# First block of x scaled in halves, late transposes by turns, last gain product on GpSimd: the start and the end of a one-core decoder kernel

## What is computed

```python
def rmsnorm(x, g):
    y = x * lax.rsqrt(jnp.mean(x * x, axis=-1, keepdims=True) + EPS)
    return y * g

h = rmsnorm(x, attn_norm_g)
proj = h @ w_in                     # conv, q, k, v and gate columns
...                                 # conv branch, windowed attention, gates, w_o, residual
h2 = rmsnorm(x, mlp_norm_g)
x = x + square(relu(h2 @ w_up)) @ w_down
out = rmsnorm(x, final_norm_g)      # 512 x 1024
```

## Time and profile before

| | us |
|---|---|
| median of 3 runs (lowest, highest) | 748.97 (748.92, 749.09) |
| the profiled execution | 749.23 |
| its span in the trace | 747.5 |
| TensorE busy | 740.1 (99% of the span) |
| VectorE busy | 658.7 (88%) |
| ScalarE busy | 429.3 (57%) |
| GpSimd busy | 86.0 (12%) |

### The profile page before, as it was taken

How to read it: one execution, slowest core, us unless ns; L and a number is a source line. 1 busy time by engine, 2 the same in 40 slices (tenths; PEclk the granted TensorE clock), 3 DMA queues, 4 the chain that set the end, 5 groups by cost and what they waited for, 6 DMA issues and landing times.

```text
span 747.5 us, 10674 instructions
## 1 busy us (share of the span) xinstructions
PE 740.1 (99%) x4194; PEld 649.9 (87%) x4194; DVE 658.7 (88%) x766; ACT 429.3 (57%) x555; POOL 86.0 (12%) x119
## 2 busy tenths in 40 slices
PE   8999999999999999999999999999999999999997
PEld 8898888888888888888888899889988999899985
DVE  6997788989899687989999999998699879986998
ACT  6773555553644557564658776654465455545556
POOL 1610000111122101010100101010101010100102
PEclk9999999999999999999999999999999999999999
DMA  9898223161247987778767847777677768676703
GB/s 325 240 299 275 76 65 105 57 168 58 84 133 238 307 226 200 191 225 200 250 169 178 215 121 214 175 196 198 170 188 199 179 171 216 173 202 181 208 1 114
DMA packets 68948, 134.41 MB, mean 180 GB/s; under 512 B 2653, under 2 KB 18085, under 8 KB 68901
## 3 DMA queue, kind: packets, MB, share of 16 engines
q1 hardware_dynamic: 48880, 85.23, 33.9%
q0 software_dynamic: 19808, 48.25, 30.0%
q10 hardware_dynamic: 212, 0.28, 0.1%
HBM read 127.43 MB, written 6.32 MB: 179 GB/s over the span
## 4 chain that ended last, share of the span: by engine, by line
PE 98%; DMA 1%; ACT 0%; DVE 0%; SPq 0%; issue 0%; ACTq 0%
PE pair L1094 46%; PE pair L1049 22%; PE pair L790 6%; PE pair L792 6%; PE pair L791 6%; PE pair L916 5%; PE pair L837 2%; PE pair L812 1%; PE pair L811 1%; PE pair L821 1%; DMA xn<-in_x 1%; PE pair L851 1%; PE pair L943 0%; PE pair L945 0%; PE pair L944 0%; PE pair L1000 0%
## 5 line engine op out<-in xcount | busy, mean ns | idle before, releaser
L1406 ACT ACTIVATE high<-home_raw 128x2048 fp32r<-128x2048 f32 x91 | 174.3, 1916 | 148.1 <-PE pair L1094 102.4
L2058 DVE TENSOR_TENSOR home_lo<-home_raw,high 128x2048 fp32r<-128x2048 f32 x91 | 208.5, 2291 | 34.4 <-ACT high L1406 34.1
L1094 PE MATMUL pair<-high,s_hi_tile 128*128 128x512 f32 x440 | 110.4, 391 | 0.0
L1094 PE MATMUL pair<-high,s_lo_tile 128*128 128x512 f32 x440 | 109.9, 390 | 0.0
L1094 PE MATMUL pair<-home_lo,s_hi_tile 128*128 128x512 f32 x440 | 109.7, 390 | 0.0
L1094 PEld LDWEIGHTS pair<-home_lo,s_hi_tile 128*128 128x128 f32 x440 | 82.4, 188 | 17.5 <-DVE home_lo L2058 0.4
L1094 PEld LDWEIGHTS pair<-high,s_lo_tile 128*128 128x128 f32 x440 | 82.4, 188 | 17.1
L1094 PEld LDWEIGHTS pair<-high,s_hi_tile 128*128 128x128 f32 x440 | 81.7, 188 | 17.4 <-ACT pair L1501 0.5
L790 PE MATMUL pair<-h,wgt 128*128 128x512 f32 x192 | 76.7, 399 | 0.0
L792 PE MATMUL pair<-h,wgt 128*128 128x512 f32 x192 | 75.0, 391 | 0.0
L791 PE MATMUL pair<-h,wgt 128*128 128x512 f32 x192 | 74.9, 390 | 0.0
(11 more groups left out here) (236 smaller groups left out, 1130.1 us busy)
## 6 DMA issues: line engine op xcount, KB each, us to landing
home_raw<-in_w_up SPq DMA_DIRECT2D x16, 1024.0 KB, 5.3
home_raw<-in_w_down SPq DMA_DIRECT2D x16, 1024.0 KB, 5.1
raw<-in_w_in SPq DMA_DIRECT2D x26, 512.0 KB, 4.9
home_raw<-in_w_up POOLq DMA_DIRECT2D x12, 1024.0 KB, 8.3
home_raw<-in_w_down POOLq DMA_DIRECT2D x12, 1024.0 KB, 8.5
home_raw<-in_w_in POOLq DMA_DIRECT2D x7, 1024.0 KB, 8.6
home_raw<-in_w_in SPq DMA_DIRECT2D x7, 1024.0 KB, 6.2
home_raw<-in_w_conv_out SPq DMA_DIRECT2D x4, 1024.0 KB, 5.2
```

What stands on the lines that cost most here:

```text
L1094: last = mm(pair[region(s, i)][:, b, :], a_[:, k, b * P:(b + 1) * P], w[:, k, :], start=(fresh and kind == 0 and k == 0), stop=(kind == 2 ...
L1406: a(high[n % 2][:, :], home_raw[home_of(s, name)][:, :], ACT.Copy).then_inc(m_hi, 1)
L2058: v.tensor_tensor(home_lo[home][:, :], home_raw[home][:, :], f32(high[n % 2][:, :]), ALU.subtract).then_inc(m_lo, 1)
```

## The change

Six edits, none of which changes what is computed:

1. x block 0 is scaled in two halves. VectorE's order is now: share of block 0, reciprocal and first half of block 0, share of block 1, second half of block 0, both halves of block 1.
2. The first transposes go block 0's four pairs, then block 1's four pairs, where before the blocks alternated from the third pair on.
3. The low part of M1's weight is made in three instructions (rows 0 and 1, row 2, row 3) where before it was two of two rows; N2's stays at two. TensorE waits and orders the third kind to match.
4. Block 3 is scaled in its two halves with the low part of tile 7 between them; tiles 4 to 6 come before.
5. The late transposes go (2,0) (2,1) (2,2) (3,0) (3,1) (2,3) (3,2) (3,3), and each pair of block 2 waits only for its own two tiles (`h_ready` 2n + 2).
6. At the end, the gain product of block 3 moves from VectorE to GpSimd, behind the two that it does; the early half of block 1 is scaled on VectorE (tensor_scalar) right behind block 1's late half, and no longer on ScalarE; block 3's late half is made and stored in two pieces of 256 columns, so SP issues eight stores.

```diff
-XN_PARTS = ((0, D), (0, D // 2, D), (0, D), (0, D // 2, D))
+XN_PARTS = ((0, D // 2, D), (0, D // 2, D), (0, D), (0, D // 2, D))
+        LOW_ROWS = {M1: ((0, 1), (2,), (3,)), N2: ((0, 1), (2, 3))}
+        def late_size(b):
+            return 256 if b == TB - 1 else 512
...
# SP
+            for b in range(TB):
+                for e in range(512 // late_size(b)):
+                    sp.wait_ge(out_late, b + e + 1)
+                    store(b, 512 * (1 - early(b)) + late_size(b) * e, late_size(b))
+                if b < TB - 1:
+                    sp.wait_ge(out_early[b], 1)
+                    store(b, 512 * early(b), 512)
+            sp.wait_ge(out_done, 16 * (2 * TB + 1))
...
# GpSimd
             gain(0)
             gain(1)
+            gain(3)
...
# TensorE
-            for b, n in ((0, 1), (1, 0), (0, 2), (1, 1), (0, 3), (1, 2), (1, 3)):
+            for b, n in ((0, 1), (0, 2), (0, 3), (1, 0), (1, 1), (1, 2), (1, 3)):
                 x_pair(b, n)
...
             def late_transposes():
-                pe.wait_ge(h_ready, 8)
-                x_transposes(2)
-                x_transposes(3)
+                for b, n in ((2, 0), (2, 1), (2, 2), (3, 0), (3, 1), (2, 3), (3, 2), (3, 3)):
+                    if b == 2:
+                        pe.wait_ge(h_ready, 2 * n + 2)
+                    x_pair(b, n)
...
# ScalarE
             def scale_early(b):
-                if b < 2:
-                    act.wait_ge(gained, b + 1)
-                else:
-                    act.wait_ge(gained_late, 1)
+                act.wait_ge(gained, 3 if b == 3 else b + 1)
...
             root_of(2)
-            scale_early(1)
             root_of(3)
...
# VectorE
             share_of_squares(0)
+            scale_x(0, (0,))
             share_of_squares(1)
-            scale_x(0)
-            scale_x(1)
+            scale_x(0, (1,))
+            scale_x(1, (0, 1))
...
-            q_low_half(M1, 0)
-            q_low_half(M1, 1)
-            scale_x(2)
+            for e in range(3):
+                q_low_rows(M1, e)
+            scale_x(2, (0,))
             share_of_squares(3)
-            for k in range(4, 8):
+            for k in range(4, 7):
                 tile_low(0, k)
-            scale_x(3)
+            scale_x(3, (0,))
+            tile_low(0, 7)
+            scale_x(3, (1,))
...
+            def scale_early_1():
+                dve.wait_ge(gained, 2)
+                r = res[:, 1, 512 * early(1):512 * early(1) + 512]
+                v.tensor_scalar(r, r, rms3[:, 2, 1:2], None, ALU.mult).then_inc(out_early[1], 1)
...
             factor(1)
-            gain(3)
             scale_late(1)
+            scale_early_1()
```

More of the change, by code:

```diff
@@ L403, in build @@
         ss3_ready, fin_step = sem("ss3_ready"), sem("fin_step")
-        gained, gained_late = sem("gained"), sem("gained_late")
+        gained = sem("gained")
         out_early, out_late = [sem(f"out_early{b}") for b in range(TB)], sem("out_late")
@@ L645, in _, with store @@
             sp.dma_start(gfin[:, :], bass.AP(final_norm_g.tensor, 0, [[0, P], [1, D]])).then_inc(gfin_in, 16)
[L646 to L653, removed]
-                else:
+            def store(b, c0, n):
+                sp.dma_start(out[rows_of(b), c0:c0 + n], res[:, b, c0:c0 + n]).then_inc(out_done, 16)
+            for b in range(TB):
[3 more added lines that the diff above has]
+                if b < TB - 1:
                     sp.wait_ge(out_early[b], 1)
-                    store(sp, b, early(b))
-            sp.wait_ge(out_done, 16 * 2 * TB)
+                    store(b, 512 * early(b), 512)
+            sp.wait_ge(out_done, 16 * (2 * TB + 1))
         @block.gpsimd
@@ L702, in _ @@
             store_sum(M6)
-            pool.wait_ge(q_low, 5)
+            pool.wait_ge(q_low, 6)
             add_q(N4, 1, 0, q_t4_in)
@@ L854, in x_pair @@
                     last.then_inc(xt_ready, 1)
-            def x_transposes(b):
-                for n in range(4):
-                    x_pair(b, n)
             def idle_transposes(n):
@@ L888, in q_product @@
                     elif early_:
-                        order = [(k, f) for e in range(2) for f in range(4) for k in (2 * e, 2 * e + 1)]
+                        order = [(k, f) for rows in LOW_ROWS[i] for f in range(4) for k in rows]
                     else:
@@ L896, in q_product @@
                         elif kind == 2:
-                            pe.wait_ge(q_low, at_ + 3)
+                            pe.wait_ge(q_low, at_ + 4)
                         if i in HS:
@@ L913, in q_product @@
                                 pe.wait_ge(h_ready, 4 * at_ + k + 1)
-                            elif k % 2 == 0:
-                                pe.wait_ge(q_low, 2 * at_ + k // 2 + 1)
+                            elif any(k == rows[0] for rows in LOW_ROWS[i]):
+                                pe.wait_ge(q_low, 3 * at_ + [rows[0] for rows in LOW_ROWS[i]].index(k) + 1)
                         last = mm(acc[:, f, :], w[:, k, f * P:(f + 1) * P], a_[:, k, :],
@@ L1783, in share_of_squares, with scale_x, q_low_rows @@
                                        ).then_inc(share_done, 1)
[L1785 to L1797, removed]
+            def scale_x(b, parts):
+                if 0 in parts:
+                    dve.wait_ge(root_done, b + 1)
+                    v.reciprocal(rms[:, 1, b:b + 1], rms[:, 0, b:b + 1]).then_inc(rms_step, 1)
+                    dve.wait_ge(rms_step, b + 1)
+                for e in parts:
+                    c = slice(*XN_PARTS[b][e:e + 2])
+                    v.tensor_scalar(xn[:, b, c], xn[:, b, c], rms[:, 1, b:b + 1], None, ALU.mult).then_inc(xn_ready, 1)
+            def q_low_rows(i, e):
+                at_, rows = Q_ORDER.index(i), LOW_ROWS[i][e]
+                c = cols(512 * rows[0], 512 * len(rows))
+                dve.wait_ge(q_high, 4 * at_ + rows[-1] + 1)
                 v.tensor_tensor(q_lo[i][:, c], q_raw[i][:, c], f32(q_hi[at_ % 2][:, c]), ALU.subtract).then_inc(q_low, 1)
@@ L1841, in _ @@
                 tile_low(0, k)
-            q_low_half(M1, 0)
-            q_low_half(M1, 1)
-            scale_x(2)
+            for e in range(3):
+                q_low_rows(M1, e)
+            scale_x(2, (0,))
             share_of_squares(3)
-            for k in range(4, 8):
+            for k in range(4, 7):
                 tile_low(0, k)
-            scale_x(3)
-            q_low_half(N2, 0)
-            q_low_half(N2, 1)
+            scale_x(3, (0,))
+            tile_low(0, 7)
+            scale_x(3, (1,))
+            for e in range(2):
+                q_low_rows(N2, e)
             late_low(0)
@@ L2425, in scale_late @@
                 ch = 1 - early(b)
[L2426 to L2429, removed]
+                acc, n = pair[region(STAGES - 1, N4)][:, 1, :], late_size(b)
+                for c0 in range(0, 512, n):
+                    r = res[:, b, 512 * ch + c0:512 * ch + c0 + n]
+                    v.scalar_tensor_tensor(out=r, in0=acc[:, c0:c0 + n] if b == 3 else r, scalar=rms3[:, 2, b:b + 1],
+                                           in1=gfin[:, 512 * ch + c0:512 * ch + c0 + n], op0=ALU.mult, op1=ALU.mult
+                                           ).then_inc(out_late, 1)
             for s in range(WO + 1, STAGES, 2):
```

## The result

| | before | after |
|---|---|---|
| median of 22 runs each, us (lowest, highest) | 749.13 (748.92, 750.09) | 750.21 (749.90, 750.81) |
| ratio, 95% interval | | 1.0015 (1.0009 to 1.0021) |
| profiled execution, us | 749.23 | 749.91 |
| its span | 747.5 | 748.2 |
| TensorE's last group of four matmuls starts at | 741.07 | 741.64 |

The kernel became 1.1 us slower. That is within the 1.5 us that I called no change, but clear of the noise of 22 runs, and on the other side of the forecast. The medians moved by +1.08; the two profiled executions differ by 0.7.

A forecast was written before the change was run, and what follows sets the result against it. TensorE, a solid body of work without waits, was taken as the bound, so only the ends could move: 0.29 us at the start plus 0.4 at the end, 0.7 off 748.97, gave 748.3 us, range 747.8 to 749.0.

The forecast's parts named there:

- The start's term, 0.29 us: At the start, M1's first matmul would begin at 9.04 us, not 9.33, and the gain would travel to the end.
- Low parts in three, late transposes by turns: In the first 20 us, the low parts avert a 0.1 us stall; the late transposes cost nothing, with slacks of 0.3 us.
- Costs one fixed part of an instruction: M1's low parts in three would cost VectorE one fixed part of an instruction, some 0.1 us.
- The step that failed: At the end, GpSimd's third product would start from about 736.75 us, after the fourth sum of squares, and take 2.65 us.
- The rival that came true, at 0.05: At the end, GpSimd's product holds up VectorE's last subtraction and TensorE slips 1.4 us: 749.7 us, chance 0.05.
- The rule of the page: GpSimd contends with VectorE instructions with two SBUF inputs, which would forecast 749.7 us; the prediction said the trace disagreed.
- The end's term, 0.4 us: At the end, earlier stores fill the traffic gap: 0.45 us gained, less 0.06 for 1 KB packets.

The follow-up runs named there:

- b2: a4 with four waits on long-passed semaphores added on VectorE near 20 us: 748.82 us, ratio 0.9995.
- a4: The changed kernel with one wait more, so that GpSimd's third product starts some 0.3 us later: 749.17 us, ratio 1.0000.
- a2: The kernel before with the edits of the start alone, the end as before: 749.34 us, ratio 1.0002.
- c1: The kernel before with four waits on long-passed semaphores added on VectorE near 20 us: 749.47 us, ratio 1.0005.
- c2: b2 with block 1's early half back on ScalarE and block 3's late half in one piece and one store: 748.94 us, ratio 0.9997.
- c3: b2 with block 3's late half in one piece and one store: 748.87 us, ratio 0.9996.
- a3: The kernel before with only block 3's gain product moved from VectorE to GpSimd: 750.01 us, ratio 1.0011.
- a1: The changed kernel with block 3's gain product back on VectorE: 749.70 us, ratio 1.0005.
- b3: a4 with 19 idle transposes in place of 25: 750.09 us, ratio 1.0013.
- c4: The kernel before with all edits of the end and GpSimd's third product started later: 748.92 us, ratio 0.9997.

## Why the prediction was wrong, point by point

- **What bounds the kernel**: right. In the two profiles all that changed lies in the first 19 and the last 13 us.
- **The start's term, 0.29 us**: right in size (0.28 in the profile of the change), right in its reason (the pair (1,0) gates the first high part: 8.37 - 5.78 = 2.59 us behind block 1's use, before 8.60 - 5.92 = 2.68). Short in one point: I took 6.9 us as the end of the idle transposes, from one execution. It varies by a microsecond, and with it the gain goes from 0.28 to below nothing (0.39 lost in b2).
- **Low parts in three, late transposes by turns**: right in size and reason, but the slack of 0.3 us doesn't always hold. In b2's profiled execution VectorE took 0.79 us for block 3's second half, and 0.48 in the eight others with the new start; one late transpose then starts 0.42 us behind the one before it and not 0.11, and the sixteen take 2.28 us where they take 1.97 in the earlier trace rows:

```profile
18.15 0.79 DVE L1791 TENSOR_SCALAR xn<-xn,rms 128x512 f32<-128x512 f32 x1
```

```profile
17.38 2.28 PE L857 MATMUL pair<-ident,xn 128*128 128x128 f32 x16
```

  GpSimd was issuing a DMA there from 17.87 us on; in the eight others VectorE's instruction began before GpSimd's. It may be the same taking of turns as at the end; no run tests it.
- **"Costs one fixed part of an instruction"**: that was all I charged for added instructions. Two entries more on VectorE's list bared a pause 700 us later, 0.35 us of VectorE and 0.09 to 0.18 us of the chain to the last reciprocal (2.25 in a4 against 2.16 in b2; 2.33 in a2 against 2.15 in the kernel before). The medians moved by 0.34 and 0.35 (c1, and a4 less b2), more than the chain accounts for and no more than their noise.
- **The step that failed: when GpSimd's product starts beside VectorE's last subtraction.** The forecast has it start at 736.75, "when the fourth sum of squares is there", 0.9 us behind the subtraction (735.85). That is misread by one sum. ScalarE in the kernel before:

```profile
735.42 0.19 ACT L1638 ACTIVATION_READ_ACCUMULATOR tz<-res 128x1 f32 x1
...
735.97 0.63 ACT L1638 ACTIVATE tz<-res 128x512 f32<-128x512 f32 x1
736.51 0.19 ACT L1638 ACTIVATION_READ_ACCUMULATOR tz<-res 128x1 f32 x1
```

  The fourth sum is the one that is there at 735.61, 0.24 us ahead of the subtraction; the one at 736.70 is the fifth, of block 0's late half. In the change the product started at 735.18, 0.16 us ahead of the subtraction, went first, and the subtraction took 3.40 us. Where I had put it, it would most likely have cost TensorE nothing: in a4 it starts 0.17 us behind, and the subtraction takes 2.29.
- **The rival that came true, at 0.05.** I named the place, a price (1.4 us shared, forecast 749.7) and the page that speaks for it, and gave it 0.05, since the two subtractions of the earlier trace rows had the same length with GpSimd beside the first. The length of the subtraction was the wrong half to look at, and I had the other half in my hand: "GpSimd takes 5.29/2 = 2.65 us". That mean hides two different numbers. The kernel before, GpSimd's two products taken one by one:

```profile
729.50 4.02 POOL L760 TENSOR_TENSOR res<-res,gfin 128x512 f32<-128x512 f32 x1 [29.72 <-ACT tz L1638]
...
733.48 1.32 POOL L760 TENSOR_TENSOR res<-res,gfin 128x512 f32<-128x512 f32 x1
```

  A product takes 1.3 us; the first took 4.02 because it stood still until the subtraction ended at 732.34. The two did contend, and GpSimd had lost. Nothing there said that it always would, and the last subtraction has 0.1 us to spare. That the price came near (1.1 us on VectorE, 0.99 on TensorE) is luck: 1.4 us was the rest of the subtraction behind 736.75, and what the subtraction waited for is a product of 1.40 us that started before it.
- **The rule of the page**: the Trainium skill, GPSIMD Engine Reference, section Key points, says that GpSimd contends with VectorE instructions that have two SBUF inputs. The runs agree: 3.40 us with the product ahead, 2.29 with it behind. The trace of before agreed too, in the 4.02 us; I said that it did not, from VectorE's side alone.
- **The end's term, 0.4 us**: 0.1 to 0.2 us of it in the traces (6.22 to 6.35 us from TensorE's last group to the end of the span in b2, c2 and c3, against 6.43). The gap did close, but then the whole of the data is one queue from the first store on, and the first store comes later: in b2 the scaling of block 0's late half takes 0.93 us and not 0.75, since GpSimd's product, now behind the subtraction, ends only at 739.8. The 1 KB packets of the earlier trace rows also go down to 322 GB/s and not 334; at that pace they would cost 0.12 us and not 0.06.
- **Range and chances**: 747.8 to 749.0 left out the one rival that came true. 0.05 was too little for a mechanism with a known place and no slack.

## What to carry to other kernels

An operation moved to GpSimd is not free beside VectorE: the two take turns at whole instructions, so ask which VectorE instructions with two SBUF inputs run when it starts, and whether one of them has slack of the operation's length; if not, start it just behind that one (here one wait, 1.0 us). Read the row of the event that releases it: here the fifth sum was taken for the fourth, and the order of the two instructions hangs on 0.2 us. Read a group of two one by one before using its mean as a cost: a first 4.02 and a second 1.32 are not two of 2.65, and the excess is the contention looked for. And gains of tenths at either end are easily paid back by things that an edit shifts without touching, so measure each such edit alone.

The best version here, b2, reached 748.82 us, 0.4 below its runs of the kernel before, with an interval that still holds no change (0.9986 to 1.0003).

## What the runs showed of the hardware

- GpSimd and VectorE hold each other up for whole instructions. A 128x512 product takes 1.3 us on GpSimd alone, 3.28 or 4.02 when it arrives beside a 2.29 us subtraction that goes first, and the subtraction 3.40 when the product does. Who goes first at a change of instruction is not settled: a product that arrived 0.57 us into a 1.22 us instruction of VectorE (729.50) still lost to the next one; products that arrived 0.98 and 0.97 us into such an instruction (735.18 in the change, 735.45 in a3) won.
- VectorE pauses some 0.35 us at one place of its instruction list, seen in the six kernels in which the reciprocal of 0.16 us stands before that place (the change, a1, a2, a4, b3, c1: 0.62 or 0.63 us from start to start, against 0.27). Behind an instruction of 0.69 us (b2) it doesn't show. Two entries added 700 us earlier are enough to bare it.
- The same 25 idle transposes took from 4.29 us (c4) to 5.59 us (b2), though the granted clock reads 1.00, the level of 2.4 GHz, in the rows of both paces (0.21 and 0.11 us a transpose). With 19 of them the time of the kernel spread over 3 us.
